# Experts of 64 of 512 tokens by gathered rows on VectorE, the dense expert products 448 tokens wide

## The reference, cut to what matters

```
s = einsum('nhpd,hpkd->nhpk', qry, sub_keys)        # 8 heads, 2 halves, 128 keys
s_top, i_top = top_k(s, 16); cand = s_top[..0] + s_top[..1] (16 x 16 sums)
sc, ci = top_k(cand, 16);  experts = e_a * 128 + e_b;  gw = softmax(sc)
act = gelu(einsum('td,tkd->tk', x, u_tab[experts]))
out = einsum('tk,tkd->td', gw * act, v_tab[experts])
```

## Time and profile before

| what | value |
|---|---|
| median of the runs | 3133.23 us |
| profiled execution, span from first to last instruction | 3131.8 us |
| u loop with its first scores, 977.7 to 1776 us | 798.3 us |
| v loop, 1776 to 2440 us | 664 us |
| TensorE busy over the span | 3017.0 us (96%) |
| VectorE, ScalarE, GpSimd busy | 1857.1, 1152.1, 1107.4 us |

### The profile page before, as it was taken

How to read it: one execution, slowest core, us unless ns; L and a number is a source line. 1 busy time by engine, 2 the same in 40 slices (tenths; PEclk the granted TensorE clock), 3 DMA queues, 4 the chain that set the end, 5 groups by cost and what they waited for, 6 DMA issues and landing times.

```text
span 3131.8 us, 37664 instructions
## 1 busy us (share of the span) xinstructions
PE 3017.0 (96%) x14633; PEld 1519.0 (49%) x14906; DVE 1857.1 (59%) x2815; ACT 1152.1 (37%) x1744; POOL 1107.4 (35%) x520
## 2 busy tenths in 40 slices
PE   8989989999999999999999999999999989889999
PEld 4444455445545456464665444444444445444444
DVE  6874987643375848686672255555555675579211
ACT  4334265434242333333433333333332453333222
POOL 2323411445243442524233444444444331225342
PEclk9999999999999999999999999999999989999999
DMA  4312310334132446656467655655555221113232
GB/s 159 105 61 75 104 51 28 101 114 149 54 101 95 152 141 173 188 155 205 148 187 223 226 202 202 206 203 205 203 204 175 78 79 48 57 62 111 91 109 79
DMA packets 266018, 415.56 MB, mean 133 GB/s; under 512 B 148041, under 2 KB 148233, under 8 KB 265458
## 3 DMA queue, kind: packets, MB, share of 16 engines
q1 hardware_dynamic: 265842, 413.14, 40.6%
HBM read 341.29 MB, written 69.22 MB: 131 GB/s over the span
## 4 chain that ended last, share of the span: by engine, by line
PE 81%; DVE 12%; issue 2%; ACT 2%; SPq 1%; DMA 1%; POOL 0%; DVEq 0%; ACTq 0%
PE banks L2118 21%; PE banks L2066 20%; PE banks L849 18%; PE banks L1330 5%; PE banks L2087 4%; PE banks L3714 4%; DVE conv_out L1823 2%; PE banks L2502 1%; DVE conv_out L1821 1%; PE banks L2442 1%; DVE ffn_hidden L2311 1%; PE banks L2485 1%; PE banks L3388 1%; PE banks L3244 1%; DVE ffn_hidden L2310 1%
## 5 line engine op out<-in xcount | busy, mean ns | idle before, releaser
L913 POOL TENSOR_TENSOR weights_lo<-weights_as_loaded,weights_hi 128x1024 bf16<-128x1024 f32 x501 | 1106.2, 2210 | 2000.5 <-ACT weights_hi L909 2000.5
L909 ACT ACTIVATE weights_hi<-weights_as_loaded 128x1024 bf16<-128x1024 f32 x505 | 531.1, 1053 | 1179.6 <-PE banks L2118 455.2
L2257 DVE TENSOR_TENSOR activation_lo<-activation_f,activation_hi 128x512 bf16<-128x512 f32 x128 | 277.4, 2168 | 313.4 <-ACT activation_hi L2149 313.4
L2118 PE MATMUL banks<-activation_hi,weights_hi 128*128 128x512 bf16 x1004 | 380.5, 379 | 1.1
L2118 PE MATMUL banks<-activation_hi,weights_lo 128*128 128x512 bf16 x1003 | 380.1, 379 | 1.1
L2118 PE MATMUL banks<-activation_lo,weights_hi 128*128 128x512 bf16 x1003 | 380.1, 379 | 1.1
L2066 PE MATMUL banks<-normed_lo,weights_hi 128*128 128x512 bf16 x999 | 378.5, 379 | 1.8
L2066 PE MATMUL banks<-normed_hi,weights_lo 128*128 128x512 bf16 x1000 | 378.9, 379 | 1.3
L2066 PE MATMUL banks<-normed_hi,weights_hi 128*128 128x512 bf16 x991 | 376.3, 380 | 1.7 <-ACT gelu_out L2135 0.5
L2135 ACT ACTIVATE gelu_out<-banks 128x512 f32<-128x512 f32 x128 | 76.2, 596 | 398.4 <-PE banks L2066 391.1
L2240 DVE TENSOR_TENSOR one_hot_b<-iota,pick_column 128x1024 bf16<-128x1024 bf16 x64 | 126.4, 1974 | 147.7 <-PE banks L2087 146.5
(11 more groups left out here) (525 smaller groups left out, 4998.9 us busy)
## 6 DMA issues: line engine op xcount, KB each, us to landing
weights_as_loaded<-in_u_tiles SPq DMA_DIRECT2D x128, 512.0 KB, 3.8
weights_as_loaded<-in_v_tiles SPq DMA_DIRECT2D x128, 512.0 KB, 3.4
gelu_of_dots<-gelu_out SPq DMA_DIRECT2D x128, 256.0 KB, 2.2
activation_f<-gelu_of_dots SPq DMA_DIRECT2D x128, 256.0 KB, 3.6
expert_weight<-expert_weights SPq DMA_DIRECT2D x128, 256.0 KB, 3.9
expert_weights<-weight_grid_even SPq DMA_DIRECT2D x32, 512.0 KB, 5.7
expert_weights<-weight_grid_odd SPq DMA_DIRECT2D x32, 512.0 KB, 5.6
weights_as_loaded<-in_w_xbc SPq DMA_DIRECT2D x24, 512.0 KB, 3.3
```

The source lines that it names most:

```text
L909: self.nc.scalar.activation(self.whi[:, s, :], self.wraw[:, s, :], ACT.Copy).then_inc(self.w_hi[s], 1)
L913: self.nc.gpsimd.tensor_tensor(self.wlo[:, s, :], self.wraw[:, s, :], self.whi[:, s, :], ALU.subtract).then_inc(self.w_lo[s], 1)
L2118: ins = nc.tensor.matmul(self.ps[:, c, :], v[:, j, c * P:(c + 1) * P], g[:, n % 4, :], start=n + m == 0, stop=n == NV - 1 and m == 2)
L2257: nc.vector.tensor_tensor(glo[:, j, :], gf[:, j, :], ghi[:, j, :], ALU.subtract).then_inc(S["g_lo"], 1)
```

## The change

The first 64 tokens leave the dense path. Their 128 slots make 8192 pairs of token and expert, handled as 64 rows of 128 pairs (`NR`): slot m half on partitions 0 to 63 and half on 64 to 127. For each of these rows GpSimd gathers 128 rows of u (4 KB each) with one indirect DMA into one of four buffers, and VectorE multiplies and sums them against the tokens, which TensorE has turned into banks 2 and 3 (`token_rows`); later the same with v rows, added up in `gathered_sum`. Eight small matmuls (`fold`) at the end add the two halves into the banks. The dense matmuls, GELUs, grid and stores are 448 tokens wide, groups fall from 64 to 56 and a lap from 8 to 7 groups. GpSimd's gathers stand behind tiles by a table (`gathers_after`).

```diff
-    GROUP, LAP = 8, 64
-    SPREAD_FROM = (30, 57, 85, 97)
-    TURN_AFTER = (22, 49, 76, 93)
+    GROUP, LAP = 8, 56
+    GT = 64
+    SPREAD_FROM = (31, 53, 80, 92)
+    TURN_AFTER = (25, 45, 72, 91)
+    EXP_AFTER = (14, 28, 50, 77)
+    INDEX_AFTER, PICKS_AFTER, ROW_GELU_AFTER = 17, 25, 104
+    FETCH_AFTER = 114
+    def gathers_after(self):
+        u = [19, 20, 21, 22, 24, 24, 32, 32] + [33 + 3 * i // 4 for i in range(8)] + [45, 45, 54, 54]
+        u += [55 + 3 * i // 4 for i in range(16)] + [73, 73, 82, 82] + [82 + 3 * i // 4 for i in range(16)]
+        u += [94 + 3 * i // 4 for i in range(8)]
+        v = list(range(106, 118)) + [120, 122, 124, 126] + [self.U_TILES + 2 * i for i in range(48)]
...
+                def gather(pool, r):
+                    if r == 0:
+                        pool.wait_ge(S["index_moved"], 16)
+                        pool.wait_ge(S["copied"], TT)
+                    if r >= 4:
+                        pool.wait_ge(S["rows_used"], r - 3)
+                    nc.gpsimd.indirect_dma_start(gathered[:, r % 4, :], None, u_rows if r < NR else v_rows,
+                                                 bass.IndirectOffsetOnAxis(ap=index[:, 0, r % NR:r % NR + 1], axis=0)
+                                                 ).then_inc(row_in[r % 4], 16)
                 for u in range(4, NU + NV + 4):
                     self.rest_of_weight(pool, slot(u), use(u))
+                    for r in range(2 * NR):
+                        if gather_at[r] == u - 4:
+                            gather(pool, r)
...
-                            ins = nc.tensor.matmul(self.ps[:, b, :], u[:, j, k * P:(k + 1) * P], xx[:, k, :],
+                            ins = nc.tensor.matmul(self.ps[:, b, GT:T], u[:, j, k * P:(k + 1) * P], xx[:, k, GT:T],
...
+                def token_rows():
+                    pe.wait_ge(S["tokens_turned"], 1)
+                    for c in range(DC):
+                        for half in range(P // GT):
+                            for m in range(2):
+                                ins = nc.tensor.matmul(self.ps[half * GT:(half + 1) * GT, 2 + c // 4, c % 4 * P:(c % 4 + 1) * P],
+                                                       x[m][:, c, 0:GT], ident_b[:, :], start=m == 0, stop=m == 1)
...
+                        if n == NV - 1:
+                            pe.wait_ge(S["rows_used"], 2 * NR)
+                            ins = nc.tensor.matmul(self.ps[:, c, 0:GT], row_sum[:, c * P:(c + 1) * P], fold[:, :],
+                                                   start=True, stop=True)
...
+                def row_dots(count):
+                    for r in range(used[0], used[0] + count):
...
+                        dve.wait_ge(row_in[r % 4], 16 * (r // 4 + 1))
+                        nc.vector.scalar_tensor_tensor(gathered[:, r % 4, :], gathered[:, r % 4, :], 1.0,
+                                                       self.ps[:, 2:4, :].rearrange("p b d -> p (b d)"), ALU.mult, ALU.mult,
+                                                       accum_out=row_dot[:, r:r + 1]).then_inc(S["rows_used"], 1)
...
+                def add_rows(count):
...
+                        dve.wait_ge(row_in[r % 4], 16 * (r // 4 + 1))
...
+                            ins = nc.vector.scalar_tensor_tensor(row_sum[:, :], gathered[:, r % 4, :], w, row_sum[:, :],
+                                                                 ALU.mult, ALU.add)
...
                     if t + 1 < TT:
                         search(t + 1)
...
+                        weigh_picks(t)
+                        if t == 0:
+                            keep_weights()
+                        row_dots(2)
                         select(t + 1)
+                        row_dots(2)
                     take(t)
-                    for k in range(PER):
+                    for k in range(PER - self.groups_of(t), PER):
                         one_hots(t, k)
+                        if used[0] < NR:
+                            row_dots(1)
...
+                weigh_rows()
+                add_rows(12)
                 for n in range(NV):
                     weigh(n)
                     if n:
                         weights_lo(n - 1)
+                    if n % 2 and used[0] < 2 * NR:
+                        add_rows(1)
```

More of the change, by code:

```diff
@@ L1938, in peer @@
         NP, NU, NV, G = 2 * PH, self.U_TILES, self.V_TILES, self.GROUP
[L1939 removed]
+        GT, TD = self.GT, T - self.GT
+        PER, NG, GPL = P // G, TD // G, self.LAP // G
+        NL, NR = TD // self.LAP, SLOTS * GT // P
         after = self.groups_after()
         first_group = [sum(after[:n]) for n in range(NU)]
[L1942 to L1944 removed]
+        tile_group = [sum(self.groups_of(i) for i in range(t)) for t in range(TT)]
+        last_tile = [max(n for n in range(NU) if first_group[n] < (lap + 1) * GPL and after[n]) for lap in range(NL)]
+        gather_at = [n for part in self.gathers_after() for n in part]
+        u_rows, v_rows = io["u_rows"], io["v_tiles"].rearrange("a p d -> (a p) d")
+        act_d = nc.dram_tensor("gelu_of_dots", [NU, P, TD], F32, kind="Internal").ap()
+        grid_d = nc.dram_tensor("expert_weights", [PKEYS, P, TD], F32, kind="Internal").ap()
         slot0, uses0, free0 = self.slot0, list(self.uses), list(self.n_free)
@@ L1999, in peer @@
         wt_in = [self.sem(f"weight_loaded{j}") for j in range(4)]
+        row_in = [self.sem(f"row_gathered{j}") for j in range(4)]
+        self.expert_sems = list(S.values()) + act_stored + grid_stored + act_in + wt_in
         def load_ring(sp, u):
@@ L2101, in _ @@
                         scores(n + 1)
+                    if n == TT:
+                        token_rows()
                     if n in self.TURN_AFTER:
@@ L2234, in four, with index_rows, keep_weights @@
                     return a[:, k * G:(k + 1) * G].rearrange("p (g t) -> p g t", t=4).unsqueeze(2).to_broadcast((P, 2, P, 4))
+                def index_rows():
+                    a, b = (picked[0:GT, 0, n, :].rearrange("p (m r) -> p m r", r=NR) for n in range(2))
+                    nc.vector.scalar_tensor_tensor(index[0:GT, :, :], a, float(PKEYS), b, ALU.mult, ALU.add
+                                                   ).then_inc(S["indexed"], 1)
+                def keep_weights():
+                    dve.wait_ge(S["weights"], 1)
+                    nc.vector.tensor_copy(row_weight[0:GT, :, :], picked[0:GT, 0, 2, :].rearrange("p (m r) -> p m r", r=NR)
+                                          ).then_inc(S["indexed"], 1)
@@ new lines, in weigh_rows @@
+                def weigh_rows():
+                    dve.wait_ge(S["row_gelu"], 1)
+                    dve.wait_ge(S["index_moved"], 32)
+                    nc.vector.tensor_tensor(row_weight[:, 0, :], row_weight[:, 0, :], row_dot[:, :], ALU.mult
+                                            ).then_inc(S["row_weighed"], 1)
+                    dve.wait_ge(S["row_weighed"], 1)
+                def add_rows(count):
+                    for r in range(used[0], used[0] + count):
+                        dve.wait_ge(row_in[r % 4], 16 * (r // 4 + 1))
+                        w = row_weight[:, 0, r - NR:r - NR + 1]
+                        if r == NR:
+                            ins = nc.vector.tensor_scalar(row_sum[:, :], gathered[:, r % 4, :], w, None, ALU.mult)
+                        else:
+                            dve.wait_ge(S["rows_used"], r)
+                            ins = nc.vector.scalar_tensor_tensor(row_sum[:, :], gathered[:, r % 4, :], w, row_sum[:, :],
+                                                                 ALU.mult, ALU.add)
+                        ins.then_inc(S["rows_used"], 1)
+                    used[0] += count
@@ L3015, in lay_out @@
     d["v_tiles"] = a["peer_v"][0].reshape(PKEYS, P, D)
+    d["u_rows"] = a["peer_u"][0]
     w = a["w_in_2"][0]
```

102 lines of the change are left out of this document (70 added, 32 removed).

## The result

The changed kernel takes 3169.08 us, median of 4 runs (3165.35 to 3177.54), against 3133.42 us (3127.9 to 3134.28, 4 runs) before: a ratio of 1.0125, with a 95% interval of 1.0106 to 1.0143. It is slower by 1.25%, a small difference but clear of the interval, where 1% faster was predicted, and it lies 11 us above the range.

A forecast was written before the change was run, and what follows sets the result against it. TensorE's queue was taken to bound the kernel. Savings of 175.2 us, less 109 for the new circle, 20 for clock and 15 for late weights, gave -31.2 us: 3102 us, likeliest case 3050 to 3126, 8-in-10 range 3035 to 3158.

The forecast's parts named there:

- widths, groups, tokens: TensorE in both loops: narrower products save 165.9 us, eight fewer groups 14.9, token_rows and fold add 5.6; -175.2 us.
- the new circle: u loop: tile end, rounding, gather, dot, one-hots, group, next tile; 22.0 us per two tiles against 14.6, 109 us in all.
- late weights behind grid stores: u loop: rounding waits for its tile's load while grid stores run, now inside the circle; 15 us, bounds 0 and 30.
- half clock: u loop: after idle pieces TensorE's matmuls run at 1.2 GHz instead of 2.4; 20 us, bounds 0 and 42.
- what comes on top: u loop, beyond the circle's 109 us: 20 us for the lower clock and 15 us for late weights behind grid stores.
- the circle's 5.5 us for a gather: u loop: a gather's time until its row has landed, bounds 3.8 and 7.8, chosen nearer a plain load's 3.8.
- the rival with hidden gathers: u loop: gathers hidden, VectorE alone limits groups, 17.3 us a pair of tiles against 14.6, 43 us; 3001, chance 0.17.
- The gather takes long: u loop: VectorE's one-hots hold up GpSimd's issuing, gather 7.8 us or more, circle 24.3 us; 3159 us, chance 0.15.
- the rule of the Trainium skill: GpSimd's gathers: it cannot write DMA descriptors while VectorE runs a two-port mode; would lengthen gathers, left unconfirmed by the rows.
- 448 columns cost more: Dense matmuls of both loops: 448 columns cost 0.1991 us each, 63 us more; 3165 us, chance 0.02.
- the v loop is bound: v loop: work shared by GpSimd and VectorE needs 10.1 us a pair of tiles, +48 us; 3150 us, chance 0.07.
- As good as hidden: u loop: gathers hidden, only VectorE's pace limits groups; 3001 us, range 3001 to 3050, chance 0.17.

The follow-up runs named there:

- e4: Changed kernel without gathers, dots or added rows, only the 448-wide products, grid and stores; 2965.55 us, ratio 0.9481 to before.
- e6: Changed kernel with its own gather table, grid stored in pieces of 3584 bytes instead of 224; 3107.7 us, ratio 0.994 to before.
- e5: Changed kernel with its own gather table, each weight load issued one tile earlier, ahead of grid stores; 3122.49 us, ratio 0.9983 to before.
- e8: e7 with each weight load issued one tile earlier; 2994.62 us, ratio 0.9574 to before.
- e7: Changed kernel with u gathers 3 to 4 tiles ahead of need, index copy and first gathers also earlier; 3011.24 us, ratio 0.9625 to before.

## Why the prediction was wrong, by its steps

Around the sum, in us, and in the profiled execution (3131.8 before, 3169.1 after, +37.3):

| term | predicted | measured |
|---|---|---|
| widths, groups, tokens | -175.2 | about -174 (e4's u loop 705 without its idle time, v loop 582.5) |
| the new circle | +109 | +128 (e6's idle time: waits for one-hots 122.0, the rest mostly for GELUs), 24 of it at the first groups |
| late weights behind grid stores | +15 | +57, with the late gathers (idle time of after less e6); 38 of it goes with the loads alone (after less e5) |
| half clock | +20 | +31, by subtraction: 922.2 - 705 - 185.6 |
| outside the two loops | 0 | -6, not followed up |

The sum was off by 68.5 us (-31.2 predicted, +37.3 measured). Some 42 of that are the stores' delays, 19 the circle and 11 the clock.

**Right: the widths.** The v loop's 3072 matmuls start 0.1896 us apart (1900.0 to 2482.4 us), predicted 0.1888; 582.5 us in place of 583. The u loop, free of waits, is 705 us in e4 (714.6 less 9.6), as in the prediction.

**Right: the mechanism.** The circle stands in the chain link by link. The gather was issued 3.84 us after the GELU (3.75), the dot took 1.30 (1.25), the undisturbed path 13.2 (14.7). The first group's one-hots ended at 1146.0 us, as worked out; TensorE waited 7.0 there instead of 4, since tile 31 was done earlier, and 24 in the first phase. The longest waits stand where the prediction had them, behind tiles 82 (12.5 us) and 61 (12.0).

**Right: the v loop has no new wait,** at a DMA share of 0.76 (0.80) and 260 GB/s (275). ScalarE is free there for 70% of the time by the earlier trace rows, not 65%; nothing hangs on it.

**The step that failed is "what comes on top".** There the late rounding got "a mean wait of 1 us or so, 15 us, bounds 0 and 30". Stores cost 57 us of waits and, by e6's u loop, 65 us with the clock. Two things were mis-sized, and the second is a term that the prediction had elsewhere, in the circle's 5.5 us for a gather. The rounding of an odd tile is 5 to 6 us late, not 1 (1390.11 against 1384.96 if on time). And the gather, priced apart at 5.5 us from rows without stores beside it, takes 6.5 to 8.1 us from its issue to the dot while stores are under way and 4.1 to 4.9 us elsewhere; the median of 6.1 us for the u rows hides both. Each alone makes the path 18 to 19 us in place of 14.7. The prediction had the row for it: a DMA share of 1.04 in a stretch with such stores. It applied it to the weight tiles alone and took 1 us from a queue that the ring of four had been hiding.

**The circle itself was short by a little.** Its 109 us measured 128 in e6. The prediction gave each turn of two tiles 22.0 us, and in e6 most took 20.7 to 22.2. Those of tiles 32, 54, 58 and 89 took 25.2 to 26.3: there two groups behind one tile wait, 7 us for the first and 2.3 for the second, although the second row has landed. That is VectorE's pace, 4.35 us for a dot and one-hots against 2.02 for a group on TensorE, and the prediction had it only in the rival with hidden gathers. Tiles 60 to 62 took 27.8 us, because the second group needs the gather behind tile 61 itself; that is the 6 us more which the prediction gave it. In most turns a tile at the lower clock takes some 6.4 us instead of 4.53, which the sum has under half clock. In the change, with the stores' delays, the turns of tiles 58 and 60 took 30.7 and 33.7 us.

**The rivals.** "The gather takes long" came nearest (3159 given, 3169 measured), with the other cause: it blamed GpSimd's issuing, held up by VectorE. GpSimd spent 0.95 us on issuing a gather in the median, and the gather landed late beside stores:

```profile
L2091 POOL DMA_INDIRECT gathered_rows<-in_u_rows,expert_index x64: 933/952/2828, 1088.1 to 1753.2; - x64
...
DMA to landing us min/median/max: 4.4/6.8/8.4
```

The first line is count, ns min/median/max; the landing is that of the gathers of both loops. An issue did take longer beside VectorE's work: 1.2 to 1.8 us beside one-hots (1.77 us at 1169.20), 2.8 us twice, beside operations of 3.2 and 4.1 us. But that adds under 1 us to a path, and VectorE stood idle while the late gathers behind tiles 58, 60, 62 and 88 were issued, in 0.95 us each. So the rule of the Trainium skill (SBUF — State Buffer, "SBUF: two separate sides") on VectorE's two-port modes, weighed in the prediction, is not what made them late; whether it holds beyond these sizes, no run here shows. "448 columns cost more" and "the v loop is bound" are out. "As good as hidden" would have been right with another table: e8 is 2994.6, and that rival had 3001. The closeness is partly luck, since e8 has the earlier loads too, which that rival did not have; e7 without them is 3011.

## What to carry to other kernels

When a change makes a queue depend on a transfer that is itself issued behind that queue's earlier work, give it lead first: the same gathers and dots cost 208 us of u loop when most stood one tile ahead of their group, and 50 when they stood three or four tiles ahead and the first ones began earlier. Price every link of such a circle from rows of the stretch in which it runs, with the DMA traffic that is there at the time, not from the median landing of the whole kernel. And small-piece stores do harm through whoever shares the DMA engines with them: look for a share near 1 at a modest GB/s.

## What the runs showed of the hardware

- An indirect gather of 128 rows of 4 KB took 0.95 us of GpSimd. The instruction took 1.2 to 1.8 us while VectorE made one-hots. From its start to the dot it was 4.1 to 4.9 us when nothing disturbed it, 6.5 to 8.1 us beside grid stores of 224-byte pieces.
- 220 GB/s filled 0.69 of the DMA engines' time in one stretch and 0.96 in one with such stores; with the stores in pieces of 3584 bytes, 246 GB/s filled 0.72. SyncE took 2.33 us to issue two stores in small pieces and 2.42 us for the load behind them, 0.93 and 0.66 us with the long pieces. In the v loop, the small pieces of e6's loads raised the share over 400 us from 0.80 to 0.89 at 272 GB/s and changed nothing: the loop took 582.5 us, as in the change, and its tiles are fetched four ahead.
- VectorE's one-hot of 0.69 us took 2.61 while GpSimd worked, so a late rounding or gather also lengthens the one-hots that fall on GpSimd's work: dot and one-hots 4.4 us alone, 6.4 with it beside them.
